# A two-block float32 transformer on one core: the first stage and both attentions put in another order

## What is computed

```python
# first block
mod = c @ w_ada + b_ada                      # shift, scale, gate
h = rmsnorm(x, g) * (1 + scale) + shift      # x is scaled by its own root mean square
proj = h @ w_in    # sb_q sb_k sb_v sb_z c_q c_kv k_rot mla_z g_a g_b
o_a = stick_breaking_attention(sb_q, sb_k, sb_v)        # 8 heads of 64
y_a = (o_a * silu(sb_z)) @ w_branch_a
q = rmsnorm(c_q) @ w_uq ; kv = rmsnorm(c_kv) @ w_ukv    # latent attention
y_b = (latent_attention(q, kv) * silu(mla_z)) @ w_branch_b
x = x + gate * ((sigmoid(g_a) * y_a + sigmoid(g_b) * y_b) @ w_out)
x = rmsnorm(x)
# second block
proj = rmsnorm(x) @ w_in_2     # gated delta rule (with a causal conv), forgetting attention
x = x + concat(o_g, o_f) @ w_out_2
x = x + (silu(gate) * up) @ w_down_2          # feed-forward, gate, up = rmsnorm(x) @ w_gate_up_2
x = x + sigmoid(rmsnorm(x) @ w_ple_gate_2) * (p @ w_ple_proj_2)
return rmsnorm(x)
```

## Time and profile before

| | |
|---|---|
| median of three runs | 1244.1 us (1243.17 to 1246.06) |
| profiled execution, its span | 1243.0 us, 1241.2 us |
| TensorE busy | 1193.9 us, 96% of the span, 6528 matmuls |
| VectorE, ScalarE, GpSimd busy | 57%, 41%, 7% |
| mean granted TensorE clock | 0.995 of full speed |
| bytes moved | 118.22 MB, mean 95 GB/s |

### The profile page before, as it was taken

One profiled execution on the slowest core, in us unless ns is written; L12 is line 12 of the kernel. 1 busy time (PEld: TensorE's weight loads), 2 busy tenths in 40 slices (PEclk: granted clock), 3 DMA queues, 4 the chain that ended last, 5 costly groups with the idle time before them and its releaser, 6 DMA issues.

```text
span 1241.2 us, 15961 instructions
## 1 busy us (share of the span) xinstructions
PE 1193.9 (96%) x6528; PEld 961.9 (77%) x6528; DVE 701.4 (57%) x1097; ACT 503.1 (41%) x803; POOL 91.5 (7%) x72
## 2 busy tenths in 40 slices
PE   5899999999999999999999989999999999999996
PEld 4787767777777788887777888878888888888885
DVE  3752664449556677366887785364444444433356
ACT  5444443364453455323356445252332232322244
POOL 0191010013000010000000200000000000000000
PEclk9899999999999999999999999999999999999998
DMA  7841332212211243331112101123223232433322
GB/s 300 320 131 57 115 118 85 65 58 86 69 51 55 96 138 98 121 119 39 64 52 73 46 3 36 38 96 104 86 101 100 88 102 98 134 104 96 112 81 73
DMA packets 35593, 118.22 MB, mean 95 GB/s; under 512 B 3936, under 2 KB 6112, under 8 KB 35520
## 3 DMA queue, kind: packets, MB, share of 16 engines
q1 hardware_dynamic: 33024, 111.03, 26.9%
q0 software_dynamic: 1392, 4.72, 1.2%
q10 hardware_dynamic: 1104, 1.45, 0.3%
HBM read 112.99 MB, written 4.19 MB: 94 GB/s over the span
## 4 chain that ended last, share of the span: by engine, by line
PE 81%; DVE 10%; ACT 6%; issue 2%; DMA 1%; POOL 0%; DVEq 0%; ACTq 0%
PE pb L654 79%; DVE wlo L1813 2%; ACT fP L1533 1%; PE pb L740 1%; ACT whi L1337 1%; DVE xT L1813 1%; ACT mP L1533 1%; PE pb L906 1%; DVE mnm L2042 1%; DMA vec<-vec_d 1%; DVE gq L1816 1%; DVE fP L2056 1%; ACT Y L1337 1%; DVE mP L2032 1%; ACT hhi L1337 0%
## 5 line engine op out<-in xcount | busy, mean ns | idle before, releaser
L654 PE MATMUL pb<-hlo,whi 128*128 128x512 f32 (+2 forms) x1056 | 409.3, 394 | 7.5 <-DVE wlo L1813 4.3
L654 PE MATMUL pb<-hhi,wlo 128*128 128x512 f32 (+2 forms) x1056 | 411.1, 389 | 5.3 <-DVE wlo L1813 3.4
L654 PE MATMUL pb<-hhi,whi 128*128 128x512 f32 (+2 forms) x1056 | 410.2, 388 | 0.0
L1813 DVE TENSOR_TENSOR wlo<-raw,whi 128x1024 fp32r<-128x1024 f32 (+1 forms) x178 | 217.2, 1225 | 105.6 <-ACT whi L1337 104.2
L654 PEld LDWEIGHTS pb<-hlo,whi 128*128 128x128 f32 (+1 forms) x1056 | 198.5, 188 | 55.6 <-DVE wlo L1813 8.3
L654 PEld LDWEIGHTS pb<-hhi,wlo 128*128 128x128 f32 (+1 forms) x1056 | 198.2, 188 | 47.7 <-DVE wlo L1813 5.0
L654 PEld LDWEIGHTS pb<-hhi,whi 128*128 128x128 f32 (+1 forms) x1056 | 198.2, 188 | 41.3
L1337 ACT ACTIVATE whi<-raw 128x1024 fp32r<-128x1024 f32 (+1 forms) x178 | 181.6, 1034 | 83.2 <-PE pb L654 69.0
L654 PE MATMUL pb<-alo,whi 128*128 128x512 f32 x176 | 68.5, 389 | 0.0
L654 PE MATMUL pb<-ahi,wlo 128*128 128x512 f32 x176 | 68.5, 389 | 0.0
L654 PE MATMUL pb<-ahi,whi 128*128 128x512 f32 x176 | 68.5, 389 | 0.0
(11 more groups left out here) (360 smaller groups left out, 1622.8 us busy)
## 6 DMA issues: line engine op xcount, KB each, us to landing
raw<-w_all SPq DMA_DIRECT2D x173, 512.0 KB, 3.5
adab<-ada_d SPq DMA_DIRECT2D x12, 512.0 KB, 10.3
raw<-w_all SPq DMA_DIRECT2D x10, 384.0 KB, 3.1
xT<-xn_d SPq DMA_DIRECT2D x4, 512.0 KB, 12.2
gbt<-ada_d SPq DMA_DIRECT2D x4, 512.0 KB, 8.9
ple_scratch<-zs SPq DMA_DIRECT2D x8, 256.0 KB, 12.5
xT<-x_d POOLq DMA_DIRECT2D x8, 256.0 KB, 3.2
out_d<-xT SPq DMA_DIRECT2D x6, 256.0 KB, 2.7
```

The lines of the kernel that those rows point to most:

```text
L654: return e.matmul(out, lhs, rhs, start=start, stop=stop, skip_group_check=True)
L1813: return e.tensor_tensor(out, a, b, op)
```

## The change

The same instructions are issued, with a few exceptions in which operation works on which PSUM bank; what changes is their order on each engine.

- SyncE, first stage: w_ada 4 is loaded ahead of sbq 2, and w_ada 6 and 7 ahead of sbq 3.
- ScalarE, first stage: sbq 0 is converted after output block 3 of p, rsx is made after block 4 in place of 5, sbq 1 is converted after block 6; then sbq 2, the first `modulated`, sbq 3, the others.
- VectorE, first stage: the low parts of p and of pp 0 come ahead of the wait for `vec`; `turn` moves from b = 1 to b = 2, behind w_ada 2 and 3; sbq 2 is converted after w_ada 4; the low part of block 0 and then sbq 3 come in b = 2.
- Stick-breaking attention: c_kv is normed after the copy of sz 0; ScalarE makes four silus in place of eight, and the other four behind the eight tanh in the latent attention.
- Latent attention, last pair: wa 4 is projected ahead of the product with v; `comb` and `comb_high` follow.
- Forgetting attention: the second spread row goes to bank 6; the projection is taken out of its bank ahead of the weight conversion.
- wo2: weights gt 0 are converted at m = 5 (before: m = 6), up 0 at 6 (7), gt 1 at 7 (after the loop); VectorE adds residual m ahead of low part and sum m-1, and makes those of block 7 behind the loop.

```diff
--- before.py
+++ after.py
@@ -524,14 +524,12 @@
             load(2)
             for t_ in range(4):
                 e.dma_start(xn[:, t_, :], xn_d[128 * t_:128 * t_ + 128, :]).then_inc(XIN[t_].sem, 16)
-            load_ada(2)
-            load(3)
-            load_ada(3)
-            load(5)
-            for n in range(4, 6):
+            for n in range(2, 8):
                 load_ada(n)
+                if n in (2, 3, 4):
+                    load(n + 1)
             load(6)
-            for n in range(6, 14):
+            for n in range(8, 14):
                 load_ada(n)
             load(7)
             for n in range(14, 16):
@@ -953,8 +951,11 @@
                     mla_qk(h + 2)
                     next(fb)
                 T.wait_ge(*VB(3))
+                if pr == 3:
+                    next(fb)
                 softmax_pv("m", pr)
-                next(fb)
+                if pr < 3:
+                    next(fb)
             for _ in fb:
                 pass
 
@@ -1004,9 +1005,10 @@
                 return mm(PB[b][:, :], sel, rhi[:, :], False, stop)
 
             def make_cb(h):
-                bank(7)
-                spread(7, 64 + h, True, True).then_inc(CBM.sem, 1)
-                free[7] = [CB(h)]
+                b = 6 if h == 1 else 7
+                bank(b)
+                spread(b, 64 + h, True, True).then_inc(CBM.sem, 1)
+                free[b] = [CB(h)]
 
             def filler_q():
                 for m in range(12):
@@ -1388,17 +1390,21 @@
                 copy(zs[:, m, :], PB[m % 4][:, :], scale=0.5).then_inc(ZPLE.sem, 1)
                 if 0 < m < 5:
                     x_square(m - 1)
-                if m == 5:
+                if m == 3:
+                    conv("sbq", 0, 0)
+                if m == 6:
+                    conv("sbq", 1, 0)
+                if m == 4:
                     A.wait_ge(*XSQ(3))
                     A.wait_ge(*EPSR())
                     e.activation(rsx[:, :], rsx[:, :], ACT.Ln, bias=eps_c, scale=1.0 / D).then_inc(RSQ.sem, 1)
                     A.wait_ge(*RSQ(("x", "ln")))
                     e.activation(rsx[:, :], rsx[:, :], ACT.Exp, scale=-0.5).then_inc(RSQ.sem, 1)
-            conv("sbq", 1, 0)
-            modulated(0)
-            conv("sbq", 3, 0)
-            for b in range(1, NB):
+            conv("sbq", 2, 0)
+            for b in range(NB):
                 modulated(b)
+                if b == 0:
+                    conv("sbq", 3, 0)
 
             conv("sbq", 3)
             for m in range(4):
@@ -1483,7 +1489,7 @@
                 next(fa)
                 if pr == 3:
                     e.preload_act_table_set(SILU)
-                    for m in range(8):
+                    for m in range(4):
                         A.wait_ge(*ZE(m))
                         e.activation(zs[:, m, :], zs[:, m, :], ACT.Silu).then_inc(SIL.sem, 1)
                     e.preload_act_table_set(EXPLN)
@@ -1552,6 +1558,9 @@
                         for k in range(8):
                             A.wait_ge(*(GAE(k) if k < 6 else GA67(k)))
                             e.activation(gax[:, k, :], gax[:, k, :], ACT.Tanh, scale=0.5).then_inc(TGA.sem, 1)
+                        for k in range(4, 8):
+                            A.wait_ge(*ZE(k))
+                            e.activation(zs[:, k, :], zs[:, k, :], ACT.Silu).then_inc(SIL.sem, 1)
                         e.preload_act_table_set(EXPLN)
                     if m == 7:
                         for k in range(4):
@@ -1582,9 +1591,11 @@
                 if pr < 3:
                     softmax_exp("m", h + 2)
                 next(fb)
-                if pr > 1:
-                    comb_high((0, 1, 2) if pr == 2 else (3,))
+                if pr == 2:
+                    comb_high((0, 1, 2))
                 next(fb)
+                if pr == 3:
+                    comb_high((3,))
             for _ in fb:
                 pass
 
@@ -1738,7 +1749,7 @@
             conv("wo2", 3)
             for m in range(8):
                 if m:
-                    conv("wo2", max(m, min(m + 3, 5)))
+                    conv("wo2", *((m, LOOK + 1) if m > 4 else (min(m + 3, 5),)))
                 high("w", m, V_FN)
                 square("w", m)
 
@@ -1851,34 +1862,37 @@
             e.memset(epsc[:, 2:3], math.log(128 ** -0.5))
             e.memset(epsc[:, 4:5], EPS * EPS)
             e.memset(epsc[:, 3:4], math.pi / 2).then_inc(EPSR.sem, 1)
+
+            for k in range(2):
+                low(("p", k), plo[:, k, :], pf[:, k, :], phi[:, k, :])
+            conv("pp", 0, 0)
+
             V.wait_ge(*VEC())
             e.tensor_scalar(sc8[:, 0:8], vec[:, V_BA + 8:V_BA + 16], 1.0, None, ALU.add).then_inc(DVS.sem, 1)
             V.wait_ge(*DVS.tick())
-
-            for k in range(2):
-                low(("p", k), plo[:, k, :], pf[:, k, :], phi[:, k, :])
-            conv("pp", 0, 0)
-
             for b in range(NB):
                 if b == 1:
                     conv("pp", 1, 0)
+                if b == 2:
                     V.wait_ge(*CST())
                     V.wait_ge(*RSQ(("x", "exp")))
                     for t_ in range(4):
                         t = e.tensor_scalar(turn[:, t_, :], ident, rsx[:, t_:t_ + 1], None, ALU.mult)
                     t.then_inc(DIAG.sem, 1)
-                if b == 2:
                     conv("sbq", 1, 0)
                 for n in (2 * b, 2 * b + 1):
                     V.wait_ge(*ADAIN[n % 12](n))
                     ada(n, ada_slot(n))
                     if n == 4:
-                        conv("sbq", 3, 0)
+                        conv("sbq", 2, 0)
+                if b == 2:
+                    low(("1", 0), hlo[:, 0, :], tmpf[:, 0, :], hhi[:, 0, :])
+                    conv("sbq", 3, 0)
                 V.wait_ge(*ADA(2 * b + 1))
                 tt(mod[:, b:b + 1], mod[:, b:b + 1], vc(V_BA + b), ALU.add)
                 stt(sc8[:, b:b + 1], mod[:, 8 + b:9 + b], sc8[:, b:b + 1], vc(V_NG + b), ALU.add, ALU.mult
                     ).then_inc(MODS.sem, 1)
-                if b:
+                if b > 1:
                     low(("1", b - 1), hlo[:, b - 1, :], tmpf[:, (b - 1) % 2, :], hhi[:, b - 1, :])
             low(("1", 7), hlo[:, 7, :], tmpf[:, 1, :], hhi[:, 7, :])
 
@@ -1939,12 +1953,13 @@
                 conv("kr")
                 rope("kr", 0, 7, proj("kr"))
                 yield
-                latent_normed("kv", 3, 2, V_KN)
                 for m in range(8):
                     n = ("sz", m) if m < 4 else ("mz", m - 4)
                     V.wait_ge(*proj(*n))
                     V.wait_ge(*PLST(7))
                     e.tensor_copy(zs[:, m, :], PB[7][:, :]).then_inc(ZE.sem, 1)
+                    if m == 0:
+                        latent_normed("kv", 3, 2, V_KN)
                     conv(*n)
                     yield
                 for m in range(6):
@@ -2116,8 +2131,12 @@
                     next(fb)
                 elif pr == 2:
                     mla_max(h + 2, fb)
-                comb(pr)
-                next(fb)
+                if pr < 3:
+                    comb(pr)
+                    next(fb)
+                else:
+                    next(fb)
+                    comb(pr)
             for _ in fb:
                 pass
 
@@ -2213,17 +2232,17 @@
             e.tensor_scalar(fv[:, 2, :], PB[2][:, :], nat[:, 2, 100:101], None, ALU.mult).then_inc(FV2.sem, 1)
             for h in range(2):
                 V.wait_ge(*CBM(h))
-                e.tensor_scalar(cbt2[:, h, :], PB[7][:, :], -1.0, None, ALU.mult).then_inc(CB.sem, 1)
+                e.tensor_scalar(cbt2[:, h, :], PB[7 - h][:, :], -1.0, None, ALU.mult).then_inc(CB.sem, 1)
 
             def filler_q():
                 for m in range(12):
-                    conv("gqkv", m)
                     x, y = cbuf[:, m % 2, :], gq[:, m, :]
                     V.wait_ge(*proj("gqkv", m))
                     V.wait_ge(*CZERO())
                     if m > 1:
                         V.wait_ge(*GQ(m - 2))
                     tt(x[:, 3:S + 3], PB[CONV_BANK[m % 3]][:, :], rs2, ALU.mult).then_inc(CVE.sem, 1)
+                    conv("gqkv", m)
                     V.wait_ge(*CVE(m))
                     e.tensor_scalar(y, x[:, 3:S + 3], vc(V_CV + 4 * m + 3), None, ALU.mult).then_inc(DVS.sem, 1)
                     for j in range(3):
@@ -2383,11 +2402,14 @@
 
             for m in range(8):
                 if m:
-                    conv("wo2", max(m, min(m + 3, 5)))
+                    conv("wo2", *((m, LOOK + 1) if m > 4 else (min(m + 3, 5),)))
                 V.wait_ge(*proj("wo2", m))
                 residual("w", m, m)
-                gained("w", m, V_FN)
-                squared("w", m)
+                if m:
+                    gained("w", m - 1, V_FN)
+                    squared("w", m - 1)
+            gained("w", 7, V_FN)
+            squared("w", 7)
 
             conv("gt", 0)
             for j in range(FFB):
```

## The result

The kernel after takes 1235.5 us, median of four runs (1233.8 to 1237.1), against 1244.6 us for the kernel before, four runs beside it (1243.2 to 1246.1): ratio 0.9927, 95% interval 0.9909 to 0.9944, 9.1 us less. A second set of five runs beside fifteen of before gave 1235.5 against 1244.1, ratio 0.9934 (0.9921 to 0.9946). The forecast was 1238.9 with a range of 1235.0 to 1243.0: inside, near its lower end. The profiled execution took 1237.1 us (span 1235.3), 5.9 us less than the profiled one of before, where the sum of the prediction was 5.2.

A forecast was written before the change was run, and what follows sets the result against it. TensorE, busy 96% of the span, bounds the kernel; only 47 us idle and slow-clock stretches are for sale. Terms -4.0 + 0.9 + 0.8 - 1.4 - 0.2 - 1.7 + 0.4 = -5.2 take 1243.0 to 1237.8, median 1238.9; range 1235.0 to 1243.0.

The forecast's parts named there:

- wo2: Second output projection: low part 7 ready some 0.4 us later, TensorE's wait 1.4; +0.4 us, bounds -1.0 and +1.3.
- First stage: Up to the sbq group: sbq 3 issued at 25.8, landed at 30.5, group passing its first block at 32.85; -4.0 us.
- only 0.3 us is left of the 2.8 won at the start: First stage: rsx taken up at about 23.8 instead of 24.13, since ScalarE now stops for sbq 0's load.
- The clock: At the sbq group's start: low clock loses 1.4 us, so the gain is 4.0 in all, 5.4 if not low.
- Rival A: Sbq group's start: clock already at 2.4 GHz, 1.4 us more won, 1237.5 us; chance 0.22.
- c_kv's norm: Stick-breaking attention: norm behind sz 0's copy makes VectorE wait, conversion late by 0.9; +0.9 us, bounds 0 and +2.3.
- Silus: Split silus: 0 in the last stick-breaking pair (bounds 0 to -1.3), +0.8 us in latent attention (0 and +2.1).
- Last latent pair: Latent attention: TensorE's 1.4 us wait for copies of turned weights filled by wa 4; -1.4 us, bounds 0 and -1.4.
- Second spread row: Forgetting attention, bank 6: 1.0 us wait goes, but scores wait for ScalarE's third v copy; -0.2 us, bounds 0 and -1.0.
- Projection ahead of conversion: Forgetting attention: four waits for cbuf, 1.7 us, go; -1.7 us, bounds -1.7 and -0.7.

The follow-up runs named there:

- e10: Kernel before with one edit: VectorE's wait for `vec` moved behind the low parts of p; 1240.7 us against 1244.1, ratio 0.9976.
- e9: Kernel after with the load of sbq 3 ahead of w_ada 6 and 7, its low part ahead of w_ada 5; 1233.1 us against 1244.4 for before.
- e11: e9 with the copy of the fourth block of v moved from ScalarE to VectorE; 1232.8 us against 1244.1 for before.
- e3: Kernel after with unread matmuls, 6 ahead of the transposition of x and 13 ahead of block 0's sbq 3 matmuls; 1234.7 us against 1244.1 for before.
- e12: e11 with unread matmuls, 6 ahead of the transposition of x and 7 ahead of block 0's sbq 3 matmuls; 1232.5 us against 1244.1 for before.
- e5: Kernel after with c_kv's norm put back ahead of VectorE's copy of sz 0; 1234.8 us against 1244.4 for before, ratio 0.9926.
- e1: Kernel before with the first-stage edits alone; 1239.6 us against 1244.1, ratio 0.9965.
- e6: Kernel before with one edit: forgetting attention's projection copy ahead of the weight conversion on VectorE; 1242.2 us against 1244.4, ratio 0.9984.
- e4: Kernel after with all eight silus back in the last stick-breaking pair; 1235.4 us, where after has 1235.5.
- e2: Kernel after with its first-stage edits undone; 1239.2 us against 1244.1 for before, ratio 0.9965.

## Why the prediction came out right, and by how much it did not

**Luck in the sum.** The median lies 0.5 us inside the low end of the range, and the way there was another than the range supposed. That end stood for a full clock at the group and good ends in wo2 and the silus (by its own terms 1237.5 - 1.4 - 0.8 = 1235.3). What was measured is a first stage near its forecast and later edits at -3.9 in place of -1.2: the norm, the silus, the copies of the projection and wo2 all came out better than priced. Two slips besides: 0.60 x 3.7 is 2.2, not 2.3, and the chances given for a faster kernel add up to 0.81, not 0.80.

**First stage: the sum right, its make-up not seen.** The start of the group was forecast within 0.1 us, and each time on the way (9.3, 25.8, 30.5) within 0.35. But I wrote "only 0.3 us is left of the 2.8 won at the start" without asking what the other order would give. e10 gives it: 2.9 of the 4.1 come from the wait for `vec` alone, and the rest of the rewrite first gives away 1.9 at rsx. A kernel with the early rsx and the early sbq 3 at once was not tried.

**The clock.** The forecast took 4.0 as the full gain of the stage, which supposes that the low clock costs the group what it did before, 1.5 us; it cost 2.9, since the low stretch fell almost whole on the group's matmuls, and the pair of traces kept 2.8. That sized the term wrong for one execution. For the median it is the other way round. In before's order three traces end the stage at 0, +1.32 and +1.38, and e10, which has before's order from rsx on, has the same 0.72 at the group; in after's order six traces end it at -2.83 to -5.24, -3.6 in the middle. From the middle of the one to the middle of the other it is 4.9 us, not 2.8, and with the later steps (-3.9, or -3.0 with the gated-delta loss) this gives 7.9 to 8.8 us, near the 8.6 to 9.1 of the medians. So of the 3 us between the traces and the medians about two thirds (4.9 less 2.8) are this, by an estimate from three and six traces: before's profile happened to be an early one (seven slow matmuls at its start where two others had ten and eleven, and in that order rsx follows the projection, so they delay all; they make about half of the 1.3), and after's was the one with the lowest clock of six. The runs say the same: before's profiled execution, 1243.0, is 1.1 under the median of its kernel, and after's, 1237.1, is the slowest of its four. The part on the slow matmuls at the start was not tested by itself. Rival A, a full clock at the group, came true in one of the six traces and half true in four. Over all traces the low clock follows the idle stretch ahead of the group in nine of ten where that stretch is as the two kernels have it, and in none of four where it is shortened to 1.9 us (e9, e11) or holds unread matmuls (e3, e12).

The Trainium skill (TensorE: Matmul & The Clock Gate, What's actually happening) says the throttled state is the default and that how many matmuls are slow differs between runs. This case shows it: between five (e3) and twelve (e12) matmuls with 0.63 us each, 0.43 us apart, at the start of the fourteen traces. Behind the idle stretch ahead of the group the same is seen again: one piece of 113 matmuls in 22.3, 23.9 or 25.1 us.

**c_kv's norm: wrong (+0.9, measured 0).** The wait was priced, the instruction behind it was not looked at. It had run beside GpSimd's subtraction and got 0.97 us shorter behind the copy (e5). The row of 2.37 us stood in the earlier trace rows, for two instructions of a kind that takes 0.7 each elsewhere. The Trainium skill (SBUF — State Buffer, Who interferes with whom) says that a VectorE instruction with two inputs in SBUF contends with a GpSimd instruction that reads SBUF, and that what they contend for is an exclusive lock. The trace of e5 agrees: GpSimd's subtraction ends at 164.96, the first of the two norm instructions, begun at 163.79, ends 0.55 us behind that and takes 1.71 us, and the second, with GpSimd done, takes 0.74. The same 1.71, 0.55 and 0.74 stand in all five traces with the norm ahead of the copy (before, e1, e5, e6, e10), and 0.74 or 0.75 for both in the nine others.

**Silus: +0.8 right in the latent attention (0.6), 0 wrong in the stick-breaking one.** The bound was 0 to -1.3 and I took 0, since VectorE waits for TensorE there; the wait for spl, which ends last at that place, got 0.5 shorter. With the silus back in one place (e4) both steps are gone and the median does not change.

**Last latent pair:** -1.4 forecast, -1.43 measured. **Second spread row:** the wait moved to ScalarE's copies of v as forecast, and all of the 1.0 went into it (1.10 us, 0.8 forecast; 0 measured, -0.2 forecast). e11 shows that part of it can be had: 0.43 by moving one copy.

**Projection ahead of conversion: too small (-1.7, measured -2.6).** The step took the idle total of the earlier trace rows as the price. For three of the four waits it tells less than half; the start-to-start times of the same matmuls would have given 0.44 each.

**wo2: wrong by a little (+0.4, measured 0).** The wait for hlo is 0.7 in two parts, 0.4 the longer, where I expected 1.4 in one.

**Gated delta rule: not in the sum.** In both traces of after the clock falls to 0.5 behind the waits near 710 us and costs 0.8 to 0.9. Whether it belongs to this order of work or is chance stays open: e1, e2, e6 and e10 don't have it, and e3, e11 and e12 lose 1.5 to 2.0 some 35 us later instead. The waits themselves, 0.6 and 0.9 us near 710 and 0.4 and 0.8 near 745, are there in the traces with the full clock too (e4, e9).

## What to carry to other kernels

Before a rewrite of many orders, price its smallest edit alone: one wait, moved behind a few instructions, was worth 3.4 of the 8.6 us. Price a wait by the start-to-start time of the matmuls around it, not by the idle figure, and look at what runs beside an instruction that you move. Before a load is moved forward in its queue, ask what it takes by itself from issue to landing (e9). In this kernel, bound by TensorE, an idle stretch has a second price, the clock behind it, which differs between executions of the same code; compare medians, and in one trace take the clock's share out first.

## What the hardware showed that was not expected

- In before's trace the granted clock of the stretch from 14 to 16 us (columns as above) reads 1.00 while its matmuls start 0.43 us apart, where later ones start 0.23 apart. The durations show a slow start that the clock column does not. The records of the clock in the trace only begin at 15.94 us, just where the spacing falls from 0.43 to 0.23 (at 14.70 in after's trace, again at that place), and a time without a record is printed as 1.00:

```profile
14.00:16.00 2.00, 2.00 (x6) 1.60 (x5) 1.97 (x5) 0.60 (x1) 0.00 (x0) 1.00 1.03 418
```

- Closing or shortening the idle stretch ahead of the group (e3, e9, e11, e12) left the clock full there in each of the four traces. In three of them it was low at another place, near 745 us, at 1.5 to 2.0 us; in e9 it was not. Whether the one has to do with the other is not shown.
- Matmuls that nobody reads, in a stretch that was idle, cost nothing that the medians can tell (e12 against e11). The clock was full behind them in both traces (e3, e12); it was full without them in e4, e9 and e11 too, so no trace proves that they are what kept it up.
